# Dilated attention in a two-layer block on one core: the query tiles of each head taken in descending order

## Chip, core and metric

The kernel runs as one program on one core of a Trainium2 chip. The metric is the device time of one execution in microseconds (us), given as the median of several runs. The engines are called PE (TensorE, matrix products), DVE (VectorE), ACT (ScalarE), POOL (GpSimd) and SP (SyncE, which issues most transfers). Each engine takes its instructions strictly in the order in which they are written; they meet only at semaphores.

## The reference, cut to what matters

The reference is a chain of transformer layers over 512 tokens of width 1024. The stage that the change touches is the dilated attention of the last layer: 4 heads of width 128, and for each head three groups of queries q (three windows with dilations 1, 4 and 16) that share the keys k and the values v. For one head h and one tile of 128 query rows the kernel computes, with only the keys up to the tile's own last row:

```
for t in range(4):                       # tile of 128 query rows, n = 128 * (t + 1) keys
    z0 = q0[h, t] @ k[h, n-256:n].T      # window 0: distance 0..128   (128 keys for t = 0)
    z1 = q1[h, t] @ k[h, 0:n].T          # window 1: distance divisible by 4
    z2 = q2[h, t] @ k[h, 0:n].T          # window 2: distance divisible by 16
    z  = scale * (masked z0, z1, z2)
    p  = exp(z - max z)                  # one maximum and one sum over all three windows
    p  = (p0 + p1 + p2) / sum(p)         # n columns
    y[h, t] = p @ v[h, 0:n]
```

The result of a head is then multiplied by a gate (z3T) and goes into the output product (wout3), which sums over the heads. So tile t = 0 has one key tile, t = 3 has four.

## The kernel before

The program is one fixed list of instructions for each engine, written out by hand. Weights come in as slabs; each is split into a high part by ACT (w_hi) and a low part by POOL (w_lo, raw minus w_hi), and a product is three matmuls (high by high, high by low, low by high).

The dilated attention has 16 units, u = 48 to 63 in the program's count (U_D = 48), here unit 0 to unit 15: unit number = 4 h + position in the head. A unit passes through the engines so:

- PE, `d_logits`: three products into three of banks 0 to 5 (two sets, taken in turn). They wait for the minimum of the unit two before (semaphore at_neg).
- DVE, `unit_least` (L2448 in the trace): mask, scale and running minimum; it writes 128 x (256 + 2n) numbers into the buffer prob3 (four buffers), or 384 columns for t = 0. For t = 2 it is two instructions, since the window pieces aren't one regular pattern.
- ACT (L1916): exponential in place, with the sum.
- POOL (L704, L706): adds window 1 and 2 (n columns), then adds window 0 (at most 256 columns).
- DVE, `unit_probs` (L2460, L2462): reciprocal, then the scaling of n columns.
- PE, `attn_transposes` (L887): t + 1 transposes into bank 6.
- ACT, `copy_probs` (L1527): bank 6 to prob3T (two buffers).
- PE: t + 1 products with v into bank 7, one quarter of the bank for a query tile. They start three steps after the logits for the transposes (LAG_T = 3), four for the products (LAG_OUT = 4).
- After the four units of a head DVE multiplies bank 7 by z3T (L2476, prob_y), and makes y_hi (L2478) and y_lo (L2479). The first product of the next head into bank 7 waits for L2476 (at_y).

The loops on all engines count `step` from 0 to 15 or 19. In a step PE does logits of unit `step`, transposes of unit `step - 3`, products of unit `step - 4`. DVE takes `unit_probs` of unit `step - 2` ahead of `unit_least` of unit `step` where step % 4 is 0 or 3, and behind it otherwise. On POOL four quarters of a w_lo slab (`lo_quarter`, L564 in the trace) are written ahead of the sums of units 8, 9, 12 and 13. On ACT one split of a weight slab follows the exponential of unit 6. From step 16 on PE has no logits, and `head_products` (12 matmuls of 512 columns for a head, in parts) of the output product fill in.

The trace gives nearly all matmuls the line of the helper `mm`, L715; logits read as `banks<-k3T,q3T`, products with v as `banks<-prob3T,v`, head products as `banks<-w_hi,y_hi` and the like. Each matmul of the program whose operands are plain f32 shows as two records.

Of the kernel before, what the change touches and what calls it, by code (L numbers as in the profile page):

```python
# [26 lines left out]
P = 128  # L27
S = 512
NT = S // P
# [124 lines left out]
def head_and_tile(n):  # L154

    return 2 * (n // 8) + n % 2, n % 8 // 2
# [3 lines left out]
LAG_T, LAG_OUT = 3, 4  # L160
# [65 lines left out]
def _program(nc, A, ctx):  # L226
# [3 lines left out]
    def place(name, kib, words, dtype=F32, parts=P):  # L230
        return nc.alloc_sbuf_tensor_at(name, [parts, words], dtype, offset=SB0 + int(kib * 1024))

    def arena(name, kib, words, dtype=F32, parts=P):
        return place(name, ARENA + kib, words, dtype, parts)
# [115 lines left out]
    prob3 = [arena(f"prob3{a}", 64 + 6 * a, 3 * S) for a in range(4)]  # L350
    prob3T = [place(f"prob3T{a}", 80 + 2 * a, S) for a in range(2)]
# [188 lines left out]
    def _(pool):  # L540
# [82 lines left out]
        for u in range(32):  # L623
            h, t = head_and_tile(u)
            n = (t + 1) * P
# [70 lines left out]
        for step in range(16):  # L696
            if step in (8, 9, 12, 13):
                lo_quarter(BASE["wout3"] + 1, (8, 9, 12, 13).index(step))
            u, t = 48 + step, step % 4
            n = (t + 1) * P  # L700
            n0 = min(n, 256)
            buf = prob3[u % 4]
            pool.wait_ge(at_exp, u + 1)
            pool.tensor_tensor(buf[:, S:S + n], buf[:, S:S + n], buf[:, S + n:S + 2 * n], ALU.add).then_inc(w_sum, 1)  # L704
            pool.wait_ge(w_sum, 2 * step + 1)
            pool.tensor_tensor(buf[:, S + n - n0:S + n], buf[:, S + n - n0:S + n], buf[:, S - n0:S], ALU.add).then_inc(w_sum, 1)  # L706
# [6 lines left out]
    def _(pe):  # L713
# [168 lines left out]
        def attn_transposes(u, src, ntiles):  # L882
            pe.wait_ge(at_norm, u + 1)
            if u >= 1:
                pe.wait_ge(at_trc, u)
            for kt in range(ntiles):
                ins = pe.transpose(banks[:, 6, kt * P:(kt + 1) * P], src[:, kt * P:(kt + 1) * P], const("ident"))  # L887
            ins.then_inc(at_tr, 1)
# [28 lines left out]
        U_C, U_A, U_D = 0, 16, 48  # L917
        for step in range(16 + LAG_OUT):
            if step < 16:
                h, t = divmod(step, 4)  # L920
                attn_logits(U_C + step, lambda u: mm(banks[:, 4 + u % 2, 0:N_MEM], cqT[:, h * S + t * P:h * S + (t + 1) * P],
                                                     mkT[:, h * N_MEM:(h + 1) * N_MEM], True, True))
            if 0 <= step - LAG_T < 16:
                u = step - LAG_T
                attn_transposes(U_C + u, prob[(U_C + u) % 4], 2)
            if step >= LAG_OUT:
                u = step - LAG_OUT
                h, t = divmod(u, 4)
# [58 lines left out]
        for step in range(32 + LAG_OUT):  # L987
            if step < 32 and step % 2 == 0:
                pair_logits(step)
            if 0 <= step - LAG_T < 32:  # L990
                u = U_A + step - LAG_T
# [66 lines left out]
        for step in range(1, 8 + 2):  # L1058
# [15 lines left out]
            if step <= 8:  # L1074
                h = step - 1
# [143 lines left out]
        for step in range(4 + 1):  # L1219
            if step < 4:  # L1220
                h = step
# [6 lines left out]
            if step >= 1:  # L1228
                h = step - 1
# [110 lines left out]

        def d_logits(u):

            h, t = divmod(u - U_D, 4)
            n = (t + 1) * P
            for w in range(3):
                k0 = max(0, n - 256) if w == 0 else 0
                c0 = 256 if (w, t) == (0, 3) else 0
                ins = mm(banks[:, 3 * (u % 2) + w, c0:c0 + n - k0], q3T[:, (4 * w + h) * S + t * P:(4 * w + h) * S + (t + 1) * P],
                         k3T[:, h * S + k0:h * S + n], True, True)
            return ins  # L1350
# [14 lines left out]
        for step in range(16 + LAG_OUT):  # L1365
            if step == 17:
                head_products(0, (2,))
            if step == 18:
                pe.wait_ge(at_neg, U_D + 16)
                head_products(0, (3,))  # L1370
            if step == 19:
                head_products(1, range(2))
            if step in (1, 3):
                wait_emptied(EV_A["z3"] + (step + 1) // 2, EV_V["z3"] + (step + 1) // 2)
            if step < 16:
                attn_logits(U_D + step, d_logits)
            if 0 <= step - LAG_T < 16:
                u = U_D + step - LAG_T
                attn_transposes(u, prob3[u % 4][:, S:2 * S], (u - U_D) % 4 + 1)
            if step == 16:  # L1380
                pe.wait_ge(at_neg, U_D + 15)
                head_products(0, range(2))
            if step >= LAG_OUT:
                u = U_D + step - LAG_OUT
                h, t = divmod(step - LAG_OUT, 4)
                pe.wait_ge(at_trc, u + 1)
                if t == 0:
                    pe.wait_ge(at_y, h)
                for kt in range(t + 1):
                    ins = mm(banks[:, 7, t * P:(t + 1) * P], v3[:, kt * HALF + h * P:kt * HALF + (h + 1) * P],  # L1390
                             prob3T[u % 2][:, kt * P:(kt + 1) * P], kt == 0, kt == t)
                ins.then_inc(at_out, 1)
# [8 lines left out]
    def _(act):  # L1401
# [121 lines left out]
        def copy_probs(u, dst, n, tr=None):  # L1523
            act.wait_ge(at_tr, u + 1)
            if u >= 2:
                act.wait_ge(at_out, u - 1)
            act.activation(dst[:, 0:n], banks[:, 6, 0:n], ACT.Copy).then_inc(at_trc, 1)  # L1527

        U_C, U_A, U_D = 0, 16, 48
# [54 lines left out]
        for step in range(16 + LAG_OUT):  # L1584
            index_relus(step - 1)
            if 0 <= step - LAG_T < 16:
                u = U_C + step - LAG_T
# [3 lines left out]
            if (step - LAG_OUT) % 4 == 3 and step >= LAG_OUT:  # L1591
                h = (step - LAG_OUT) // 4
# [13 lines left out]
        for step in range(32 + LAG_OUT):  # L1606
            if 0 <= step - LAG_T < 32:
                u = U_A + step - LAG_T
# [18 lines left out]
        for step in range(8 + 2):  # L1627
# [12 lines left out]
            for n, c in enumerate((LATER, FIRST)):  # L1640
# [3 lines left out]
                if 1 <= step <= 8:  # L1644
                    h = step - 1
# [127 lines left out]
        for step in range(4 + 2):  # L1773
            if step < 4:
                h = step
# [12 lines left out]
            if step >= 2:  # L1788
                h = step - 2
# [114 lines left out]
        for step in range(16 + LAG_OUT):  # L1904
            if 0 <= step - LAG_T < 16:
                u = U_D + step - LAG_T
                copy_probs(u, prob3T[u % 2], ((step - LAG_T) % 4 + 1) * P)
            if step < 16:
                u = U_D + step
                n = (step % 4 + 1) * P  # L1910
                buf = prob3[u % 4]
                b = word_of(u)
                packed = buf[:, S - min(n, 256):S + 2 * n]
                least = b + 1 if step % 4 == 2 else b
                act.wait_ge(at_neg, u + 1)
                act.activation(packed, packed, ACT.Exp, bias=negmax[:, least:least + 1], scale=-1.0,  # L1916
                               accum_out=total[:, b:b + 1]).then_inc(at_exp, 1)
            if step == 6:
                split_hi(0, "wout3", 0)
# [4 lines left out]
    def _(dve):  # L1924
# [87 lines left out]
        U_C, U_A, U_D = 0, 16, 48  # L2012
# [45 lines left out]
        for step in range(16 + LAG_OUT):  # L2058
            index_sums(step - 2)
            if step < 16:  # L2060
                u = U_C + step
# [7 lines left out]
            if (step - LAG_OUT) % 4 == 3 and step >= LAG_OUT:  # L2069
                h = (step - LAG_OUT) // 4  # L2070
# [48 lines left out]
        for step in range(32 + LAG_OUT):  # L2119
            if step < 32:  # L2120
                u, t = U_A + step, head_and_tile(step)[1]
                n = (t + 1) * P
# [188 lines left out]
        for step in range(4 + 2):  # L2311
            if step < 4:
                h = step
# [5 lines left out]
            if step >= 2:  # L2319
                h = step - 2  # L2320
# [5 lines left out]
            if 1 <= step <= 4:  # L2326
                h = step - 1
# [11 lines left out]
            if step >= 2:  # L2339
                h = step - 2  # L2340
# [87 lines left out]
            dve.tensor_tensor(part, flat[:, 2048 + 1024 * s:3072 + 1024 * s], part, ALU.mult).then_inc(ev_v, 1)  # L2428
        dve.wait_ge(rp_Tc, 16)
        def unit_least(step):  # L2430
            u, t = U_D + step, step % 4
            n = (t + 1) * P
            n0 = min(n, 256)
            b = word_of(u)
            dve.wait_ge(at_log, u + 1)
            dve.wait_ge(at_tr, u - 3)
            buf, b0 = prob3[u % 4], 3 * (u % 2)
            if t == 3:
                parts = [(buf[:, 256:256 + 1280], flat[:, b0 * 512 + 256:b0 * 512 + 1536], dil[:])]
            elif t == 2:  # L2440
                parts = [(buf[:, S - 256:S], banks[:, b0, 0:256], dil[:, 0:256]),
                         (buf[:, S:S + 2 * n].rearrange("p (w c) -> p w c", w=2), banks[:, b0 + 1:b0 + 3, 0:n],
                          dil[:, 256:].rearrange("p (w c) -> p w c", w=2)[:, :, S - n:S])]
            else:
                parts = [(buf[:, S - n:S + 2 * n].rearrange("p (w c) -> p w c", w=3), banks[:, b0:b0 + 3, 0:n],
                          dil[:].rearrange("p (w c) -> p w c", w=5)[:, 0:5:2, 256 - n:256])]
            for i, (packed, logits, mask) in enumerate(parts):
                ins = dve.tensor_tensor_reduce(out=packed, in0=logits, in1=mask, scale=-scale_c,  # L2448
                                               scalar=3.0e38 if i == 0 else negmax[:, b:b + 1], op0=ALU.add, op1=ALU.min,
                                               accum_out=negmax[:, b + i:b + i + 1])  # L2450
                if i < len(parts) - 1:
                    link(ins)
            ins.then_inc(at_neg, 1)

        def unit_probs(step):
            u, t = U_D + step - 2, (step - 2) % 4
            n = (t + 1) * P
            b, buf = word_of(u), prob3[u % 4]
            dve.wait_ge(at_exp, u + 1)
            link(dve.reciprocal(inverse[:, b:b + 1], total[:, b:b + 1]))  # L2460
            dve.wait_ge(w_sum, 2 * (step - 1))
            dve.tensor_scalar(buf[:, S:S + n], buf[:, S:S + n], inverse[:, b:b + 1], None, ALU.mult).then_inc(at_norm, 1)  # L2462

        for step in range(16 + LAG_OUT):
# [7 lines left out]
            if (step - LAG_OUT) % 4 == 3 and step >= LAG_OUT:  # L2472
                h = (step - LAG_OUT) // 4
# [45 lines left out]
```

## Time and profile before

| | |
|---|---|
| median of 3 runs | 1568.92 us (1567.63 to 1568.95) |
| time of the profiled execution | 1567.16 us |
| its span, first to last instruction | 1565.4 us |
| PE busy | 1529.0 us, 98% |
| DVE, ACT, POOL busy | 700.2, 596.7, 693.3 us |
| granted TensorE clock | 1.0 of full speed |
| dilated attention, first logits to last head product | 1435.9 to 1491.9 us |

PE is busy for nearly the whole span, so what counts is where it waits. The stage of the change is the last 56 us but one; behind it come the second half of the output product and a gated addition.

### The profile page before, as it was taken

What the parts mean: (1) busy time and instruction counts of PE and PEld (TensorE: products, weight loads), DVE (VectorE), ACT (ScalarE), POOL (GpSimd) and SP (SyncE); (2) the same over time, 40 slices, a digit from 0 to 9 for tenths busy, and PEclk for the clock granted to TensorE, in tenths of its full rate; (3) what the DMA queues carried; (4) which work ended last, traced back from release to release, by engine and by line L of the source; (5) the groups of instructions that cost most, each with busy time, mean ns of one, the idle gap of its engine ahead of it and who ended that gap; (6) DMA issues with size and microseconds to landing.
All of it is one profiled execution on the core that took longest, in us unless ns stands there. A gap on an engine that the chain in (4) does not pass through costs nothing.

```text
span 1565.4 us, 19693 instructions
## 1 busy us (share of the span) xinstructions
PE 1529.0 (98%) x7585; PEld 1252.2 (80%) x7585; DVE 700.2 (45%) x1147; ACT 596.7 (38%) x908; POOL 693.3 (44%) x312
## 2 busy tenths in 40 slices
PE   7999999999999999999999999999999999999898
PEld 6877966868888888888888887888878888887687
DVE  4157855382243326656655005630035346445733
ACT  5353245573223315221222114422344444455452
POOL 5423365233555545534444344444432434454632
PEclk9999999999999999999999999999999999999999
DMA  7323311102333332333332225443421232322021
GB/s 233 112 75 112 105 54 48 41 21 76 87 97 100 114 108 68 108 107 86 102 107 81 108 82 70 98 106 91 126 68 54 81 108 81 95 81 81 28 69 67
DMA packets 144966, 138.26 MB, mean 88 GB/s; under 512 B 7760, under 2 KB 118224, under 8 KB 144892
## 3 DMA queue, kind: packets, MB, share of 16 engines
q1 hardware_dynamic: 140676, 130.79, 29.0%
q10 hardware_dynamic: 4216, 6.45, 1.3%
q8 instruction: 51, 0.84, 0.2%
q14 instruction: 23, 0.19, 0.0%
HBM read 135.09 MB, written 2.13 MB: 88 GB/s over the span
## 4 chain that ended last, share of the span: by engine, by line
PE 89%; DVE 3%; ACT 3%; POOL 3%; issue 1%; DMA 1%; SPq 0%; DVEq 0%; ACTq 0%; POOLq 0%
PE banks L715 86%; POOL w_lo L564 2%; PE banks L741 2%; PE banks L887 1%; DMA raw<-in_w_mem_kv 1%; ACT w_hi L1427 0%; PE banks L1303 0%; DVE prob L2448 0%; POOL prob L704 0%; DVE resid L2212 0%; ACT k L1854 0%; ACT junk L1693 0%; POOL prob L706 0%; ACT junk L1686 0%; DVE head_ms L2410 0%
## 5 line engine op out<-in xcount | busy, mean ns | idle before, releaser
L547 POOL TENSOR_TENSOR w_lo<-raw,w_hi 128x2048 fp32r<-128x2048 f32 x104 | 481.3, 4628 | 602.3 <-ACT w_hi L1427 602.3
L715 PE MATMUL banks<-h_hi,w_hi 128*128 128x512 f32 (+1 forms) x904 | 348.0, 385 | 2.4 <-DVE h_lo L1991 0.9
L715 PE MATMUL banks<-h_hi,w_lo 128*128 128x512 f32 (+1 forms) x904 | 340.4, 377 | 0.0
L715 PE MATMUL banks<-h_lo,w_hi 128*128 128x512 f32 (+1 forms) x904 | 340.1, 376 | 0.0
L1427 ACT ACTIVATE w_hi<-raw 128x2048 fp32r<-128x2048 f32 x126 | 238.8, 1896 | 214.8 <-PE banks L715 209.4
L715 PEld LDWEIGHTS banks<-h_hi,w_hi 128*128 128x128 f32 x904 | 169.9, 188 | 42.5 <-issue 9.7
L715 PE MATMUL banks<-w_hi,h_hi 128*128 128x512 f32 (+1 forms) x544 | 199.3, 366 | 0.0
L715 PE MATMUL banks<-w_hi,h_lo 128*128 128x512 f32 (+1 forms) x544 | 198.1, 364 | 0.0
L715 PE MATMUL banks<-w_lo,h_hi 128*128 128x512 f32 (+1 forms) x544 | 198.1, 364 | 0.0
L715 PEld LDWEIGHTS banks<-h_hi,w_lo 128*128 128x128 f32 x904 | 169.7, 188 | 32.2
L715 PEld LDWEIGHTS banks<-h_lo,w_hi 128*128 128x128 f32 x904 | 170.0, 188 | 29.0
L564 POOL TENSOR_TENSOR w_lo<-raw,w_hi 128x512 fp32r<-128x512 f32 x84 | 113.2, 1367 | 96.1 <-ACT w_hi L1427 91.0
L715 PEld LDWEIGHTS banks<-w_hi,h_hi 128*128 128x128 f32 x544 | 102.7, 189 | 16.7 <-issue 0.9
L715 PEld LDWEIGHTS banks<-w_hi,h_lo 128*128 128x128 f32 x544 | 102.6, 189 | 16.4
L715 PEld LDWEIGHTS banks<-w_lo,h_hi 128*128 128x128 f32 x544 | 102.7, 189 | 15.8
L2253 DVE TENSOR_TENSOR f_lo<-ff_prod,f_hi 128x512 f32 x22 | 102.8, 4675 | 4.3 <-DVE f_hi L2251 2.9
L1717 ACT ACTIVATE ff_sig<-banks 128x512 f32<-128x512 f32 x22 | 13.2, 600 | 175.8 <-PE banks L715 175.8
L1972 DVE TENSOR_REDUCE meansq<-sumsq 128x1 f32<-128x2 f32 (+4 forms) x19 | 2.9, 153 | 151.1 <-ACT junk L1686 130.4
L715 PE MATMUL banks<-w_hi,f_lo 128*128 128x512 f32 x176 | 68.5, 389 | 0.0
L715 PE MATMUL banks<-w_hi,f_hi 128*128 128x512 f32 x176 | 68.5, 389 | 0.0
L715 PE MATMUL banks<-w_lo,f_hi 128*128 128x512 f32 x176 | 68.5, 389 | 0.0
L1666 ACT ACTIVATE gate<-banks,col 128x512 f32<-128x512 f32 x24 | 16.5, 689 | 130.5 <-PE banks L715 130.5
(310 smaller groups left out, 2330.9 us busy)
## 6 DMA issues: line engine op xcount, KB each, us to landing
raw<-in_w_in SPq DMA_DIRECT2D x56, 512.0 KB, 4.0
raw<-in_w_ffn_in SPq DMA_DIRECT2D x44, 512.0 KB, 4.8
raw<-in_w_in_a SPq DMA_DIRECT2D x32, 512.0 KB, 5.7
raw<-in_w_ffn_out SPq DMA_DIRECT2D x22, 512.0 KB, 4.0
raw<-in_w_ple_gate SPq DMA_DIRECT2D x16, 512.0 KB, 4.6
raw<-in_w_in_b SPq DMA_DIRECT2D x16, 512.0 KB, 4.3
raw<-in_w_mem_kv SPq DMA_DIRECT2D x8, 512.0 KB, 5.7
raw<-in_w_out SPq DMA_DIRECT2D x8, 512.0 KB, 3.6
```

What stands on the lines that cost most here:

```text
L547: pool.tensor_tensor(slot_of(w_lo, slot), slot_of(raw, slot), slot_of(w_hi, slot).bitcast(F32), ALU.subtract).then_inc(lo_made, 1)
L564: ins = pool.tensor_tensor(w_lo[:, c], raw[:, c], w_hi[:, c].bitcast(F32), ALU.subtract)
L715: return pe.matmul(out, lhsT, rhs, start=start, stop=stop, **kw)
L741: ins = pe.transpose(banks[:, transposed_bank(name, k), t * P:(t + 1) * P], rows(t)[:, k * P:(k + 1) * P], const("ident"))
L887: ins = pe.transpose(banks[:, 6, kt * P:(kt + 1) * P], src[:, kt * P:(kt + 1) * P], const("ident"))
L1427: act.activation(slot_of(w_hi, slot, words), slot_of(raw, slot, words), ACT.Copy).then_inc(hi_made, 1)
L1666: act.activation(gate[slot][:], banks[:, 2 * slot, :], ACT.Sigmoid, bias=col[:, ds(V_BGATE + KD * (s % 3) + ft, 1)]).then_inc(ev_a, 1)
L1717: act.activation(ff_sig[:], banks[:, 2 * slot, :], ACT.Sigmoid).then_inc(ev_a, 1)
L1972: link(dve.tensor_reduce(meansq[:, c], pieces, AX_X, ALU.add))
L2253: dve.tensor_tensor(lo, ff_prod[:], hi.bitcast(F32), ALU.subtract).then_inc(lo_ffn, 1)
```

## The change

The position in the head is kept, but the query tile that stands in it is reversed on every engine: position 0 is now t = 3 (four key tiles), position 3 is t = 0. The transposes and copies of a unit have the matching sizes, the wait for bank 7 stands ahead of t = 3, now the first of a head, and the number where the minimum of t = 2 lies follows that tile. Buffers, lags, the order of `unit_probs` and `unit_least`, and the steps of the w_lo quarters are as before. No instruction is added or removed.

```diff
@@ POOL
             if step in (8, 9, 12, 13):
                 lo_quarter(BASE["wout3"] + 1, (8, 9, 12, 13).index(step))
-            u, t = 48 + step, step % 4
+            u, t = 48 + step, 3 - step % 4
@@ PE, d_logits
-            h, t = divmod(u - U_D, 4)
+            h, t = (u - U_D) // 4, 3 - (u - U_D) % 4
@@ PE, loop over steps
-                attn_transposes(u, prob3[u % 4][:, S:2 * S], (u - U_D) % 4 + 1)
+                attn_transposes(u, prob3[u % 4][:, S:2 * S], 4 - (u - U_D) % 4)
...
-                h, t = divmod(step - LAG_OUT, 4)
+                h, t = (step - LAG_OUT) // 4, 3 - (step - LAG_OUT) % 4
                 pe.wait_ge(at_trc, u + 1)
-                if t == 0:
+                if t == NT - 1:
                     pe.wait_ge(at_y, h)
@@ ACT
-                copy_probs(u, prob3T[u % 2], ((step - LAG_T) % 4 + 1) * P)
+                copy_probs(u, prob3T[u % 2], (4 - (step - LAG_T) % 4) * P)
...
-                n = (step % 4 + 1) * P
+                n = (4 - step % 4) * P
...
-                least = b + 1 if step % 4 == 2 else b
+                least = b + 1 if step % 4 == 1 else b
@@ DVE, unit_least
-            u, t = U_D + step, step % 4
+            u, t = U_D + step, 3 - step % 4
@@ DVE, unit_probs
-            u, t = U_D + step - 2, (step - 2) % 4
+            u, t = U_D + step - 2, 3 - (step - 2) % 4
```

The start of the stage on PE, before (prob_182 to prob_185 are the four buffers of prob3, prob3T_186 is the first of the two prob3T):

```order
L715 MATMUL banks<-k3T,q3T 128x128 x3
L715 MATMUL banks<-k3T,q3T 128x256 x4
L715 MATMUL banks<-k3T,q3T 128x384 x2
L715 MATMUL banks<-k3T,q3T 128x256
L715 MATMUL banks<-k3T,q3T 128x512 x2
L887 MATMUL banks<-sq,prob_182 128x128
L715 MATMUL banks<-k3T,q3T 128x128 x3
L887 MATMUL banks<-sq,prob_183 128x128 x2
L715 MATMUL banks<-prob3T_186,v_167 128x128
```

The same place on PE with the change:

```order
L715 MATMUL banks<-k3T,q3T 128x256
L715 MATMUL banks<-k3T,q3T 128x512 x2
L715 MATMUL banks<-k3T,q3T 128x256
L715 MATMUL banks<-k3T,q3T 128x384 x2
L715 MATMUL banks<-k3T,q3T 128x256 x3
L715 MATMUL banks<-k3T,q3T 128x128 x3
L887 MATMUL banks<-sq,prob_182 128x128 x4
L715 MATMUL banks<-k3T,q3T 128x256
L715 MATMUL banks<-k3T,q3T 128x512 x2
L887 MATMUL banks<-sq,prob_183 128x128 x3
```

Between the first transposes and the first product with v there now stand the logits of a unit with four key tiles, where those of a unit with one key tile stood.

The border of two heads on POOL (units 7, 8 and 9; the border at units 11, 12 and 13 is alike), before:

```order
L704 TENSOR_TENSOR prob_185<-prob_185 128x512
L706 TENSOR_TENSOR prob_185<-prob_185 128x256
L564 TENSOR_TENSOR w_lo<-raw,w_hi 128x512
L704 TENSOR_TENSOR prob_182<-prob_182 128x128
L706 TENSOR_TENSOR prob_182<-prob_182 128x128
L564 TENSOR_TENSOR w_lo<-raw,w_hi 128x512
L704 TENSOR_TENSOR prob_183<-prob_183 128x256
```

The same place on POOL with the change:

```order
L704 TENSOR_TENSOR prob_185<-prob_185 128x128
L706 TENSOR_TENSOR prob_185<-prob_185 128x128
L564 TENSOR_TENSOR w_lo<-raw,w_hi 128x512
L704 TENSOR_TENSOR prob_182<-prob_182 128x512
L706 TENSOR_TENSOR prob_182<-prob_182 128x256
L564 TENSOR_TENSOR w_lo<-raw,w_hi 128x512
L704 TENSOR_TENSOR prob_183<-prob_183 128x384
```

The quarters of w_lo stand where they stood by number, but now ahead of and right behind the sums of the head's largest unit.

## Rows read from the trace of the kernel before

**Rows 1.** The page: busy time of each engine, and the chain that ended last.

```profile
PE 1529.0 (98%) x7585; PEld 1252.2 (80%) x7585; DVE 700.2 (45%) x1147; ACT 596.7 (38%) x908; POOL 693.3 (44%) x312
...
PE 89%; DVE 3%; ACT 3%; POOL 3%; issue 1%; DMA 1%; SPq 0%; DVEq 0%; ACTq 0%; POOLq 0%
```

**Rows 2.** Windows: start:end, length, busy us of PE, PEld, DVE, ACT, POOL; clock, DMA.

```profile
1435.89:1444.25 8.36, 7.35 (x34) 4.90 (x33) 5.79 (x14) 5.45 (x9) 2.84 (x5) 1.00 0.36 126
1444.25:1454.85 10.60, 9.96 (x56) 7.17 (x55) 7.40 (x22) 8.24 (x14) 7.36 (x10) 1.00 0.01 2
1454.85:1466.19 11.34, 9.62 (x54) 7.22 (x55) 9.68 (x22) 5.83 (x13) 8.71 (x10) 1.00 0.00 0
1466.19:1477.54 11.35, 10.40 (x54) 7.61 (x55) 9.68 (x22) 5.84 (x13) 8.72 (x10) 1.00 0.30 92
1477.54:1491.88 14.34, 13.06 (x70) 10.93 (x71) 6.67 (x12) 3.36 (x9) 2.07 (x2) 1.00 0.00 2
```

**Rows 3.** Timeline of PE: start us, us; in brackets idle before and releaser.

```profile
1442.87 0.33 PE L887 MATMUL banks<-sq,prob 128*128 128x128 f32 x1
...
1450.25 2.31 PE L715 MATMUL banks<-k3T,q3T 128*128 128x256 f32 x6
1452.40 0.27 PE L887 MATMUL banks<-sq,prob 128*128 128x128 f32 x1
1452.51 1.06 PE L715 MATMUL banks<-prob3T,v 128*128 128x128 f32 x8
1453.41 0.83 PE L715 MATMUL banks<-k3T,q3T 128*128 128x128 f32 x6
...
1457.29 0.55 PE L887 MATMUL banks<-sq,prob 128*128 128x128 f32 x3 [0.68 <-DVE prob L2462]
...
1466.19 0.46 PE L715 MATMUL banks<-prob3T,v 128*128 128x128 f32 x2 [1.04 <-DVE prob_y L2476]
...
1479.98 0.55 PE L887 MATMUL banks<-sq,prob 128*128 128x128 f32 x3 [1.28 <-DVE prob L2462]
...
1486.28 0.40 PE L715 MATMUL banks<-w_hi,y_hi 128*128 128x512 f32 x1
...
1491.06 0.39 PE L715 MATMUL banks<-w_hi,y_hi 128*128 128x512 f32 x1
```

**Rows 4.** Timeline of DVE.

```profile
1438.29 0.55 DVE L2448 CUSTOM_DVE_ANT_1 prob<-banks,dil 128x384 f32<-128x384 f32 x1
...
1445.69 0.42 DVE L2462 TENSOR_SCALAR prob<-prob,inverse 128x384 f32<-128x384 f32 x1 [0.94 <-POOL prob L706]
...
1452.60 1.49 DVE L2448 CUSTOM_DVE_ANT_0 prob<-banks,dil 128x1280 f32<-128x1280 f32 x1 [0.94 <-PE banks L715]
...
1456.00 1.23 DVE L2462 TENSOR_SCALAR prob<-prob,inverse 128x384 f32<-128x384 f32 x1
...
1458.70 0.65 DVE L2462 TENSOR_SCALAR prob<-prob,inverse 128x512 f32<-128x512 f32 x1
...
1463.01 1.02 DVE L2462 TENSOR_SCALAR prob<-prob,inverse 128x256 f32<-128x256 f32 x1 [0.75 <-POOL prob L706]
```

**Rows 5.** Timeline of ACT: one exponential and the read of its sum.

```profile
1454.14 1.36 ACT L1916 ACTIVATE prob<-prob,negmax 128x1280 f32<-128x1280 f32 x1
1455.40 0.18 ACT L1916 ACTIVATION_READ_ACCUMULATOR prob<-prob,negmax 128x1 f32 x1
```

**Rows 6.** Timeline of POOL around the border of heads 1 and 2.

```profile
1455.67 1.35 POOL L704 TENSOR_TENSOR prob<-prob 128x512 f32<-128x512 f32 x1 [1.68 <-ACT prob L1916]
1457.09 0.73 POOL L706 TENSOR_TENSOR prob<-prob 128x256 f32<-128x256 f32 x1
1457.79 1.27 POOL L564 TENSOR_TENSOR w_lo<-raw,w_hi 128x512 fp32r<-128x512 f32 x1
1459.03 0.63 POOL L704 TENSOR_TENSOR prob<-prob 128x128 f32<-128x128 f32 x1
...
1462.89 0.99 POOL L704 TENSOR_TENSOR prob<-prob 128x384 f32<-128x384 f32 x1
```

## The prediction

> **What bounds the kernel now.** I read the page first: PE is busy for 98% of the span and carries 89% of the chain that ended last [rows 1]. No work is added or taken away, so the change can only move PE's waits in its own stage. I therefore cut the stage into stretches, each from one head's first product with v to the next head's [rows 2]: 8.36 us to fill the pipeline, then 10.60, 11.34 and 11.35 us for three heads, and 14.34 us from the last head's first product to the last head product. The reader is to see that POOL and DVE are as loaded as PE there: 8.7 us of POOL and 9.7 us of DVE in an 11.34 us head. The first of the three has no quarter of w_lo on POOL and is 0.74 us shorter.
>
> Then the timeline of PE in that stretch [rows 3]. A row's length holds an overlap with the next one, so I take start to start. A four-key-tile unit costs 2.15 us of logits (1450.25 to 1452.40), 0.11 us for one transpose (1452.40 to 1452.51), 0.90 us for four key tiles of products (1452.51 to 1453.41). Its other sizes, read in the same way, give logits of 0.67, 1.30, 1.72 and 2.15 us for t = 0 to 3, transposes of 0.11, 0.25, 0.35 and 0.45, and products of 0.30, 0.45, 0.67 and 0.90: 9.3 us for a head. The rest of a head is waits: for the scaled probabilities (0.68 us, and 1.28 in the last head) and for the reading of bank 7 (1.04 us).
>
> Who makes these waits is on DVE and POOL. A scaling of 384 columns takes 0.42 us, but 1.23 us at 1456.00 [rows 4]. POOL's add ran from 1455.67 to 1457.02 [rows 6], and the scaling ended 0.21 us behind it. The scaling of 256 columns at 1463.01 had waited for POOL's sums, and took 1.02 us since POOL had already gone on at 1462.89 to the next unit's add, which ended at 1463.88. The scaling of 512 columns at 1458.70 ended at 1459.35, 0.29 us behind the w_lo quarter [rows 4, 6]. So **a scaling that finds POOL at work ends 0.1 to 0.3 us after POOL's instruction, by its size**, and where POOL has its next one ready, it gets there first. In the other direction the add at 1459.03 took 0.63 us, though 0.32 us of DVE's scaling were still to come; the same add without DVE beside it takes 0.46, so 0.17 us were lost.
>
> The Trainium skill says in "SBUF — State Buffer", section "SBUF: two separate sides", that such pairs of DVE and GpSimd instructions share a port pair under an exclusive lock, which whoever starts first holds for its whole instruction. The trace agrees for DVE. For POOL the rule would charge the whole 0.32 us and the row only 0.17. That difference comes three times on the path below (0.15 us each); by the rule the sum would be about 3.3 us, by the row it is 2.9.
>
> **The change, part by part.** I walked the new order through the engines with these start-to-start costs, each instruction starting at the later of its engine's last and its releaser's end. The hand-over times are read from neighbouring rows: 0.04 us DVE to ACT, 0.08 to POOL, 0.10 POOL to DVE, 0.06 to PE, 0.14 behind a copy or bank-7 read. The same walk over the old order ends at 1491.86 us, where the trace has 1491.88; none of POOL's 36 starts is off by more than 0.12 us. All matmuls, the minimum, exponential and sums exist in the trace in every size; only their neighbours are new.
>
> *Fill.* DVE's first minimum starts at 1438.29 as before [rows 4], since it waits for the gate, not PE (the larger logits from 1435.89 take 2.31 us and are ready at 1438.20). From here the larger unit costs: minimum 1.49 (1439.78); exponential with its sum 1.44, being 1.36 plus 0.18 less 0.10 of overlap [rows 5] (1441.28); POOL's sums 1.28 + 0.07 + 0.73 [rows 6] (1443.43). POOL goes straight on to unit 1's add, 1.00 us, to 1444.40. The scaling, ready at 1443.53, ends at 1444.69. PE's first transposes start at 1444.75, against 1442.87 [rows 3]: 1.88 us late. Up to the first product there then lie 0.45 (four transposes) + 2.15 (logits of unit 4) + 0.35, and no longer 1.38 us with a small wait: another 1.57. First product at 1447.70: **+3.45 us**.
>
> *Head 1.* PE's 9.3 us plus waits of 0.31 and 0.66 us for scalings: 10.28 against 10.60, **-0.32**. The wait for bank 7 is gone here, as the small last unit makes its reading early.
>
> *Head 2.* A scaling of t = 0 meets POOL's 512-column add (0.84 us of wait on PE). That of t = 3 (unit 8) is ready at 1464.39; POOL went to its w_lo quarter at 1464.26, holds it to 1465.53, and PE waits 1.01 us. Bank 7 costs 0.48. 11.63 against 11.34: **+0.29**.
>
> *Head 3.* The large unit now opens the head on DVE too: its minimum comes behind y_lo and a scaling (1471.2), its exponential ends at 1474.17, POOL's sums to 1476.42, then the quarter again ahead of the scaling, to 1477.66. PE waits 2.2 us. Behind it unit 13's sums end at 1479.60 and its scaling loses to the next add: 1.8 us. PE has 8.6 us of work in this stretch (no logits in its last step, 1.40 us of head products in), with 0.14 us of other wait 12.72 against 11.35: **+1.37**.
>
> *Tail.* The last units are small, so all that follows the last head's first product is PE's own work: products 0.90 + 0.67 + 0.45 + 0.30, transposes 0.23 + 0.11, 14 head-product tiles (the other two lie in head 3) of 0.70 us: seven of them take 4.78 us from 1486.28 to 1491.06 [rows 3], 0.68 each, and I add 0.02 for the first of a group. Together 12.46 us. Before, this stretch was 14.34 us with the 1.28 us wait: **-1.88**. The last y_lo (1489.8) lies 2 us ahead of the products that need it.
>
> The w_lo quarters end at 1477.7, 17 us before wout3's second half wants them, and PE is 89% of the chain [rows 1], all of it just behind the stage, so the shift passes on whole. Sum: 3.45 - 0.32 + 0.29 + 1.37 - 1.88 = **+2.9 us**, on the profiled execution 1567.16 to 1570.1. The median of the runs is 1.8 us above the profiled one; I add the shift to it: 1568.92 + 2.9 = **1571.8 us**, 0.18% more. What a measurement of this kernel can tell from no change is about 0.2%, 3.1 us.
>
> Where the walk is soft are the races between DVE and POOL. Moving each cost by 0.04 us at random moves the sum between 2.0 and 3.1 us, in 1 of 30 cases over 4. Without POOL's share of the collisions (a lower bound) it is 2.4.
>
> **The rivals.** *The collisions go worse (slower side).* If the misses of head 3 already come in head 2, at units 8 and 9, that head too takes 12.7 us: +1.1, and one more missed race is another 0.5 to 0.9. Against it speaks that PE has logits to do in head 2; for it that POOL's quarter at unit 9 is ready at once. It decides when the scaling of unit 8 ends after 1466.5. Total +4.0 to +4.9, 1573.4.
>
> *The scaling slips in first.* If DVE gets through between POOL's instructions at units 0, 8, 12 and 13, the first transposes come 0.67 us earlier, the others 0.94, 0.94 and 0.5: 3.0 us less, nothing is left, 1568.9. The row at 1463.01 speaks against it: DVE was released by the very instruction after which POOL went on, and came second.
>
> *Only the tail counts (faster).* PE never waits once the pipeline is full: heads of 9.3, 9.3 and 8.6 us, a fill of +3.45 and the tail of -1.88 give 3.45 - 1.3 - 2.0 - 2.8 - 1.9 = -4.5 us, 1564.4. It needs POOL's quarters to fall into POOL's waits for exponentials alone and every scaling in time, so it is decided by the waits at units 8 and 12 being under 0.3 us. POOL's 8.7 us of work in a head, nearly all in one chain with DVE and ACT, speaks against it.
>
> **How the numbers follow.** The forecast has 0.50, the worse collisions 0.27, the scaling first 0.16, the faster one 0.04, and 0.03 for nothing at all. The forecast's own spread passes 3.1 us in a quarter of its cases (0.13), giving slower 0.41, within 0.2% 0.55, faster 0.04. The range holds the forecast, most of the worse collisions and most of the case without them: 1569.3 to 1573.8.
>
> **What would show it.** PE's first L887 near 1444.7 and first product with v near 1447.7; stretches of the heads near 10.3, 11.6 and 12.7 us; scalings of 512 columns of about 1.2 to 1.4 us at units 0, 8 and 12; a wait of about 2 us ahead of the transposes of unit 12; no PE wait behind the last head's first product. The prediction is wrong if the scalings of 512 columns last 0.5 us, or if PE waits for minima (its logits) at the borders of heads, which the walk has nowhere after the start.

## The result and the profile after

| | before | changed |
|---|---|---|
| median | 1568.28 us (8 runs) | 1574.15 us (8 runs) |
| lowest to highest | 1567.19 to 1569.19 | 1571.55 to 1575.62 |
| profiled execution, span | 1565.4 us | 1571.8 us |
| granted clock, mean over the span, single runs | 1.000 to 0.999 | 0.999 to 0.996 |

The ratio is 1.0037 (95% interval 1.0028 to 1.0046): 5.9 us slower, twice the 2.9 us that I forecast, and above my range, which ended at 1573.8. The direction was right. The page of the changed kernel shows PE busy for 4 us more, though not one instruction was added [rows 1]:

```profile
PE 1533.0 (98%) x7585; PEld 1255.6 (80%) x7585; DVE 703.0 (45%) x1147; ACT 597.3 (38%) x908; POOL 694.4 (44%) x312
```

Here is the stage of the changed kernel in windows, cut as in [rows 2]: fill, three heads, tail. The columns are the same; the third number from the right is the granted clock.

```profile
1436.38:1449.92 13.54, 11.13 (x38) 6.59 (x37) 7.86 (x18) 7.23 (x11) 6.06 (x8) 0.87 0.21 78
1449.92:1460.12 10.20, 9.61 (x56) 7.23 (x55) 7.96 (x19) 7.69 (x13) 5.41 (x7) 1.00 0.01 2
1460.12:1471.74 11.62, 9.78 (x57) 7.18 (x55) 9.61 (x21) 5.99 (x13) 8.82 (x10) 1.00 0.00 0
1471.74:1485.22 13.48, 10.03 (x54) 8.02 (x55) 11.51 (x25) 6.21 (x13) 10.46 (x12) 0.93 0.26 78
1485.22:1498.23 13.01, 13.01 (x67) 11.18 (x66) 4.30 (x9) 1.92 (x6) 0.00 (x0) 0.94 0.01 1
```

Heads 1 and 2 came out at 10.20 and 11.62 us, where the prediction had 10.28 and 11.63. The fill took 13.54 (predicted 11.81), head 3 13.48 (12.72), the tail 13.01 (12.46), and these three are the stretches in which the granted clock isn't 1.00. PE's timeline of the changed kernel shows where:

```profile
1442.09 0.91 PE L715 MATMUL banks<-k3T,q3T 128*128 128x128 f32 x6
1445.26 0.75 PE L887 MATMUL banks<-sq,prob 128*128 128x128 f32 x4 [2.26 <-DVE prob L2462]
1445.80 3.96 PE L715 MATMUL banks<-k3T,q3T 128*128 128x256 f32 x6
...
1479.99 0.66 PE L887 MATMUL banks<-sq,prob 128*128 128x128 f32 x4 [0.79 <-DVE prob L2462]
1480.49 0.39 PE L715 MATMUL banks<-prob3T,v 128*128 128x128 f32 x2
1482.55 0.55 PE L887 MATMUL banks<-sq,prob 128*128 128x128 f32 x3 [1.68 <-DVE prob L2462]
...
1483.94 0.63 PE L715 MATMUL banks<-w_hi,y_hi 128*128 128x512 f32 x1
...
1485.22 1.74 PE L715 MATMUL banks<-prob3T,v 128*128 128x128 f32 x8
```

The logits of a unit with four key tiles take 3.96 us behind a wait of 2.26 us, and took 2.31 before [rows 3]. A head-product matmul takes 0.63 us (0.40 in [rows 3]), and eight records of products with v 1.74 us (1.06). Windows around the two places, with the same columns as above:

```profile
1442.99:1445.26 2.27, 0.01 (x1) 0.00 (x1) 0.86 (x3) 1.15 (x4) 2.11 (x4) 1.00 0.01 4
1445.26:1449.60 4.34, 4.34 (x11) 2.38 (x12) 1.72 (x6) 1.30 (x3) 2.85 (x5) 0.61 0.00 0
...
1480.49:1482.55 2.06, 0.38 (x5) 0.20 (x3) 0.85 (x2) 0.60 (x1) 1.90 (x4) 1.00 0.79 159
1482.55:1485.22 2.67, 2.67 (x9) 2.17 (x10) 2.56 (x7) 1.08 (x3) 1.88 (x3) 0.63 0.70 270
1485.22:1487.03 1.81, 1.81 (x10) 1.77 (x9) 0.50 (x3) 0.00 (x0) 0.00 (x0) 0.60 0.04 9
```

The reader is to see that PE is idle for most of the two stretches 1442.99:1445.26 and 1480.49:1482.55 while the clock is still granted in full, and busy throughout in the rows behind them, at a clock that has meanwhile fallen (a mean of about 0.6 over stretches that hold a piece at 1.00 and some 3 us at 0.50). The price is read from start to start. Up to the first product the fill is 1.73 us above the walk. The two head-product tiles take 2.37 us (1482.85 to 1485.22) where 1.40 were counted, and the products 1.50 (1485.22 to 1486.72) where 0.90 were: 1.57. Together 3.3 us of 5.9, and the other 2.6 are the order of the work.

### The profile page after: what moved, and what is told of

It reads as the page before. It is cut to its first block, busy times and chain, and to the rows that moved or that the text cites. A ratio compares the mean times of both kernels' runs of the same rounds, so it can differ in the third digit from the quotient of the medians.

```text
span 1571.8 us, 19693 instructions
## 1 busy us (share of the span) xinstructions
PE 1533.0 (98%) x7585; PEld 1255.6 (80%) x7585; DVE 703.0 (45%) x1147; ACT 597.3 (38%) x908; POOL 694.4 (44%) x312
## 4 chain that ended last, share of the span: by engine, by line
PE 89%; ACT 3%; DVE 3%; POOL 2%; issue 2%; DMA 0%; ACTq 0%; DVEq 0%; POOLq 0%
PE banks L715 86%; PE banks L741 2%; POOL w_lo L564 1%; PE banks L887 1%; ACT w_hi L1427 1%; POOL prob L704 1%; PE banks L1303 0%; DMA onehot<-in_c_onehot 0%; DVE resid L2212 0%; ACT k L1854 0%; DVE prob L2448 0%; POOL prob L706 0%; ACT junk L1693 0%; ACT junk L1686 0%; DVE head_ms L2410 0%
```

## Experiments

The stage starts at 1435.89 us in the earliest trace and at 1437.87 in the latest, though nothing ahead of it was changed in these kernels but e12_fill_up (more on that at the end), so I compare the stage itself in the traces: from the first logits to the last head product. Its end is the start of the last unit's products with v, plus those, plus ten tiles of head products, which take 7.07 us (1484.81 to 1491.88 before). Before it is 55.99 us, in the changed kernel 61.85. The *walk* is the prediction's, extended with each edit and always at full clock. Its 58.7 us for the changed kernel and 55.8 for before are the measure for the rows below (the prediction's own walk of before ended at 1491.86 us, a stage of 55.97). Each stage is that of one traced execution. Medians and ratios are to runs of the kernel before on the same chip.

| kernel | walk | stage | clock below 1 in the stage | median | ratio, 95% interval |
|---|---|---|---|---|---|
| changed | 58.7 | 61.85 | fill, end | 1574.15 | 1.0037 (1.0028 to 1.0046) |
| e1_fill | 58.7 | 60.24 | end | 1573.20 | 1.0032 (1.0020 to 1.0044) |
| e5_fill2 | 58.7 | 58.72 | no | 1570.12 | 1.0013 (1.0004 to 1.0022) |
| e2_hp | 58.3 | 60.04 | fill, end | 1573.05 | 1.0028 (1.0017 to 1.0039) |
| e3_both | 58.3 | 58.29 | no | 1571.21 | 1.0017 (1.0008 to 1.0026) |
| e9_wait | 58.0 | 59.71 | fill | 1572.55 | 1.0028 (1.0017 to 1.0038) |
| e6_addd | 56.1 | 58.59 | end | 1569.88 | 1.0010 (1.0001 to 1.0019) |
| e7_daaa | 58.2 | 59.60 | fill | 1571.43 | 1.0023 (1.0014 to 1.0032) |
| e4_dve | 56.7 | 59.97 | fill, end | 1571.33 | 1.0018 (1.0009 to 1.0027) |
| e10_dddd | 55.1 | 55.13 | no | 1569.78 | 1.0003 (0.9994 to 1.0012) |
| e11_aaaa | 54.9 | about 55.2 | no | 1566.62 | 0.9990 (0.9981 to 0.9999) |
| e8_best | 52.6 | 52.77 | no | 1564.31 | 0.9981 (0.9972 to 0.9990) |

**e1_fill: work in the first wait.**

```diff
+            if step == 3:
+                for _ in range(9):
+                    mm(banks[:, 7, :], h_hi[:, 0:P], h_hi[:, 0:S], True, True)
             if 0 <= step - LAG_T < 16:
                 u = U_D + step - LAG_T
                 attn_transposes(...)
```

> Changed kernel, with nine matmuls of 512 columns (results overwritten later, bank 7) put on PE ahead of the first transposes, where PE waits 2.3 us. Clock theory (the long wait lowers the granted clock, and the logits behind it run slowly: 3.96 us in place of 2.31): those logits take 2.3 us again and the whole is 1.5 to 1.9 us faster than the changed kernel, so about 4.3 us over before. Rival (the loss is all order of work: waits and collisions): the added matmuls hide at best, so 5.9 us over before, or more.

PE's timeline of e1_fill:

```profile
1444.10 2.33 PE L715 MATMUL banks<-h_hi 128*128 128x512 f32 x9
1446.66 0.66 PE L887 MATMUL banks<-sq,prob 128*128 128x128 f32 x4 [0.23 <-DVE prob L2465]
1447.15 2.31 PE L715 MATMUL banks<-k3T,q3T 128*128 128x256 f32 x6
```

The logits are back at 2.31 us, and the stage is 1.61 us shorter, by matmuls that compute nothing. The clock fell at the end of the stage alone. In the ratio to before the difference to the changed kernel is within the intervals, and the median is 0.95 us lower where 1.5 to 1.9 were expected. So the gain rests on one trace each, and a fall can also stay away by itself (e10_dddd below); the next run has more than that to show.

**e5_fill2: work in the second wait too.** This is e1_fill with, in step 16 ahead of the transposes of unit 13:

```diff
+            if step == 16:
+                pe.wait_ge(at_neg, U_D + 15)
+                pe.wait_ge(at_lo, 9)
+                for _ in range(6):
+                    mm(banks[:, 2, :], y3_hi[:, 0:P], y3_hi[:, 0:S], True, True)
```

> Kernel e1_fill, with six more matmuls of 512 columns (results overwritten later, bank 2) in step 16 ahead of the transposes of unit 13, where PE waits 1.68 us. The order of the real work is as in the changed kernel. Clock theory: the granted clock stays at 1.0, the two head-product tiles behind take 1.4 us in place of 2.4 and the next products with v 0.9 in place of 1.5, so the stage is 1.6 us shorter than in e1_fill (58.7 us from first logits to last head product, against 60.2). Rival (the slow matmuls there come from something else beside them, transfers or POOL): no shorter than e1_fill.

PE's timeline of e5_fill2:

```profile
1480.35 1.64 PE L715 MATMUL banks<-y_hi 128*128 128x512 f32 x6
1482.29 0.55 PE L887 MATMUL banks<-sq,prob 128*128 128x128 f32 x3 [0.30 <-DVE prob L2470]
...
1484.06 1.05 PE L715 MATMUL banks<-prob3T,v 128*128 128x128 f32 x8
```

The products with v take 1.05 us and no longer 1.74. The stage is 58.72 us, the walk's number for the changed order without any fall of the clock. So 3.1 of the 5.9 us were the clock, and the order itself cost 2.7. Here the runs show it too: the intervals of e5_fill2 and the changed kernel don't touch, and the medians are 4.0 us apart. Eight of the eleven runs lie between 1569.85 and 1570.22 us and three between 1571.62 and 1571.93, where none of the changed kernel's eight is under 1571.55. The traced run, 1571.66, is one of the three, with a fall of the clock 280 us ahead of the stage and none in it. Transfers ran beside these matmuls here as in the changed kernel (their share was 0.60 from 1482.60 to 1485.22), so transfers alone don't make the matmuls slow.

**e2_hp and e3_both: real work in the second wait.** Head products of tiles 0 and 1 move ahead of the transposes of unit 13; e3_both adds the fill of e1_fill.

```diff
+            if step == 16:
+                pe.wait_ge(at_neg, U_D + 15)
+                head_products(0, range(2))
             if 0 <= step - LAG_T < 16:
                 ... attn_transposes ...
-            if step == 16:
-                pe.wait_ge(at_neg, U_D + 15)
-                head_products(0, range(2))
```

> Changed kernel, with the first two tiles of head products taken ahead of the transposes of unit 13 in step 16, so that real work fills PE's second long wait. Clock theory: 1.4 us saved by the order and 1.2 to 1.6 us more because the head products and the next products with v no longer run at a lowered clock: 2.6 to 3.0 us faster than the changed kernel, 2.9 to 3.3 over before. Rival (order alone): 1.4 us faster, 4.5 over before, and the matmuls behind the transposes still show 0.56 to 0.63 us each.

> Both edits together. Clock theory: the two costs are separate and add, 4.3 to 4.8 us faster than the changed kernel, 1.1 to 1.6 over before. Rival (order alone): 1.4 us faster than the changed kernel, 4.5 over before.

e2_hp came out nearer to the rival. Its stage is 1.81 us shorter than the changed kernel's and its median 1.1 us lower, 4.4 over before, and head-product matmuls still take 0.63 us. But the slow matmuls are no longer those behind the filled wait. The clock fell one wait earlier, behind the wait of 1.98 us for unit 12, as PE's timeline of e2_hp shows.

```profile
1481.39 1.11 PE L887 MATMUL banks<-sq,prob 128*128 128x128 f32 x4 [1.98 <-DVE prob L2462]
```

My 1.4 us for the order was too high as well. In the walk it is 0.4, because the first product of the last head then waits for the reading of bank 7 (0.62 us in e3_both). The table's 58.3 us are the walk with this wait in it. The expectations went by 1.4 us, which is 57.3, so that e3_both meets 58.3 is no forecast that came true. e3_both had no fall in the stage, not even behind a wait of 1.99 us for unit 12. "Order alone, 1.4 us" is refuted by it, but so is my sum of 4.3 to 4.8: the stage is 3.6 us shorter than the changed kernel's, the median 2.9 lower.

**e9_wait: the old order with a long wait.** The kernel before, and nothing else but:

```diff
+            if step == 3:
+                pe.wait_ge(at_norm, U_D + 3)
             if 0 <= step - LAG_T < 16:
```

> The kernel before, old order throughout, with one wait added: PE's first transposes also wait for the scaling of unit 2, so that PE is idle for 3.3 us there. The walk without any effect of the clock gives a stage of 58.0 us against 55.8. Clock theory: the granted clock falls to half behind this wait although no tile is reversed, for 3 to 4 us, and what runs there takes up to twice its time; 58.0 to 59.7 us, since later waits can hide a part. Rival (the fall belongs to the descending order or its larger logits): clock 1.0 throughout, 58.0 us.

PE's timeline of e9_wait, with the logits of a unit with one key tile in the second row:

```profile
1446.17 0.43 PE L887 MATMUL banks<-sq,prob 128*128 128x128 f32 x1 [3.12 <-DVE prob L2464]
1446.40 1.49 PE L715 MATMUL banks<-k3T,q3T 128*128 128x128 f32 x6
```

1.49 us, against 0.83 in [rows 3], and a stage 1.7 us above the walk. Two windows of e9_wait behind the wait, at the lower clock:

```profile
1447.00:1448.00 1.00, 1.00 (x7) 1.00 (x6) 0.07 (x1) 1.00 (x1) 0.00 (x0) 0.50 0.00 0
1448.00:1449.00 1.00, 1.00 (x6) 0.91 (x5) 0.49 (x2) 0.91 (x4) 0.66 (x1) 0.50 0.00 0
```

None of the eight runs is less than 3.6 us above the lowest of before, where the wait alone is worth 2.2 by the walk. So the fall needs neither the descending order nor large logits; it follows the wait.

**e6_addd and e7_daaa: one part of the change alone.** All tile numbers go through one function, here for heads 1 to 3 descending (e6_addd) or head 0 alone (e7_daaa).

```diff
+ASCENDING = (0,)          # e7_daaa: (1, 2, 3)
+def tile_of(n):
+    return n % 4 if n // 4 in ASCENDING else 3 - n % 4
```

> The change on heads 1 to 3 only; head 0 keeps its ascending order. The walk gives 0.3 us over before, and waits of 2.2 and 1.8 us ahead of the transposes of units 12 and 13, so by the clock theory another 1.6 us: 1.9 over before, stage 57.7 us. Rival (all of the loss is in the descending order of every head alike): three quarters of 5.9 us, 4.4 over before.

> The change on head 0 only. The walk gives 2.4 us over before, with the 2.6 us wait ahead of the first transposes, behind which the clock falls (1.7 us more); the end of the stage is as before and the clock doesn't fall there. 4.1 over before, stage 60.0 us. Rival (as for e6_addd): a quarter of 5.9 us, 1.5 over before.

The loss doesn't spread evenly, so the rival is out. Head 0 alone costs 3.6 us of stage, with a median 2.7 us over before. The other three cost 2.6 in the profiled execution, where the clock fell already behind the 1.98 us wait for unit 12 and stayed low longer than I had counted; its runs have a median 1.1 us over before. By the walk, the order of heads 1 to 3 costs only 0.3.

**e4_dve: DVE's order reversed as well.**

```diff
-            probs_first = step % 4 in (0, 3)
+            probs_first = step % 4 in (1, 2)
```

> Changed kernel, with DVE's order reversed as well: unit_probs ahead of unit_least in steps with step % 4 of 1 and 2 in place of 0 and 3. The walk through the engines gives 2.1 us less waiting than the changed kernel, with the first wait of 2.6 us still there and one of 1.8 us ahead of unit 13's transposes. If the walk's account of waits holds and the clock falls at the same two places, it is about 2 us faster than the changed kernel, 3.8 over before. Rival (DVE's order doesn't matter, POOL's chain sets the heads): within 0.5 us of the changed kernel.

The stage is 1.88 us shorter than the changed kernel's, with both falls of the clock still there, and the median 2.8 lower. That `probs_first` was fitted to the ascending sizes, and that the change left it as it was, is thus a part of the 2.6 us of order.

**e8_best, e10_dddd, e11_aaaa: the order with its surroundings fitted.** The three have these edits in common, found by walking variants; they differ in the heads that descend: 1 to 3, all, none.

```diff
-            if step in (8, 9, 12, 13):
+            if step in (8, 11, 12, 15):          # POOL, w_lo quarters
...
-            probs_first = step % 4 in (0, 3)
+            probs_first = step % 4 in (3,)       # DVE
...
+            if step == 16:                       # PE, ahead of the transposes
+                pe.wait_ge(at_neg, U_D + 15)
+                head_products(0, range(3))
             if step == 17:
-                head_products(0, (2,))
-            if step == 18:
                 pe.wait_ge(at_neg, U_D + 16)
                 head_products(0, (3,))
...
-            if step == 16:                       # PE, behind the transposes
-                pe.wait_ge(at_neg, U_D + 15)
-                head_products(0, range(2))
```

> Kernel e6_addd (head 0 ascending, heads 1 to 3 descending) with three edits that the walk points to: unit_probs ahead of unit_least in steps with step % 4 of 3 alone, the w_lo quarters ahead of units 8, 11, 12 and 15, and the first three tiles of head products ahead of the transposes of unit 13, the fourth in step 17. The walk gives a stage of 52.6 us against 55.8 before, with no PE wait over 1.1 us, so no fall of the clock: 3.2 us faster than before. Rival (the walk misses waits once several orders change together): no faster than before.

> The three edits of e8_best with all four heads descending, as in the change. Walk 55.1 us, plus 1.7 us for the clock behind the 2.3 us wait ahead of the first transposes: stage 56.8 us, 0.8 over before. Rival (with the three edits the order doesn't matter): 52.8 us as e8_best, 3 us faster than before.

> The three edits of e8_best with all four heads ascending, as before. Walk 54.9 us, no fall of the clock: 0.9 us faster than before. If e8_best owes its gain to the three edits alone, this is 3 us faster; if to the descending heads alone, not faster at all; by the walk it needs both.

e8_best is faster than both kernels, 0.9981 (0.9972 to 0.9990) of before. The stage is 3.2 us shorter, and its longest wait is the 0.88 us that the kernel before has too. With the same three edits, no head descending gives 0.9990, all four 1.0003. The gain needs both, and descending in head 0 spoils it. The traces show where. Against e11_aaaa, e8_best has 2.8 us less from head 2's first product with v to the end (22.70 for 25.51), 0.8 less in the two stretches ahead of that, and 1.2 more in the fill, which holds the logits of head 1's large first unit. Against e8_best, e10_dddd has 2.33 us more in the fill (11.85 for 9.52) and 0.03 in all the rest. So the descending order isn't bad in itself: it is good at the end of the stage, and bad at its start, where PE has nothing else to do until the first unit has passed through four engines.

e10_dddd missed its expectation in the trace in one respect. PE waited 2.26 us ahead of the first transposes, as in the changed kernel, and the clock did not fall. Windows of e10_dddd up to that wait's end and behind it:

```profile
1437.71:1446.59 8.88, 6.47 (x25) 3.89 (x23) 6.02 (x12) 5.92 (x8) 3.21 (x4) 1.00 0.35 119
1446.59:1450.60 4.01, 4.01 (x22) 2.95 (x23) 2.46 (x5) 1.80 (x4) 2.87 (x5) 1.00 0.00 0
```

Up to that wait the instructions are those of the changed kernel. So the same wait has a fall behind it in one execution and none in another. The times fit that: two of e10_dddd's eleven runs lie near 1566.5 us, three near 1568.0 and six near 1570.0. The traced one, 1568.11, is of the middle group and has one fall, ahead of the stage. The highest group would then have both, but none of its runs has a trace.

**e12_fill_up: the wait far ahead of the stage.** Every kernel of this study but e12_fill_up has another such place in the mLSTM stage. One row of the kernel before and one of e3_both, of the same eight records behind the same wait:

```profile
1157.04 2.42 PE L715 MATMUL banks<-qk2T 128*128 128x512 f32 x8 [2.49 <-DVE wts L2318]
```

```profile
1157.10 4.07 PE L715 MATMUL banks<-qk2T 128*128 128x512 f32 x8 [2.49 <-DVE wts L2321]
```

The traces of e1_fill, e2_hp, e3_both, e5_fill2, e10_dddd and e11_aaaa have the fall there, the other seven with the wait have not. Where a kernel's times lie in two groups, the traced run is of the upper one in e5_fill2 and e11_aaaa, which have the fall, and of the lower one in before and e8_best, which have none. e7_daaa's is of its upper one, with a fall elsewhere (last section). The 25 runs of before beside e9_wait split 10 to 15 into 1567.1 to 1567.8 us and 1568.5 to 1569.3, with mean clocks of 1.000 and 0.999 (once 0.998). The edit, on e8_best:

```diff
+                if h == 1:
+                    for _ in range(4):
+                        mm(banks[:, 4, :], qk2T[:, 4 * S:4 * S + P], qk2T[:, 0:S], True, True)
                 if h:
                     pe.wait_ge(m_w, h)
```

> Kernel e8_best, with four plain f32 matmuls of 512 columns (results overwritten later, bank 4) put on PE some 280 us ahead of the dilated attention, in the wait of 2.49 us for the weights of the mLSTM stage's second head (near 1157 us). The times of e8_best lie in two groups, near 1564.1 and 1565.95 us, those of the kernel before near 1567.2 and 1569.1. If the upper group is the executions in which the clock falls behind that wait, all times lie near 1564.1 and the median is 1564.2, 4.5 us faster than before. Rival (the two groups come from somewhere else, a transfer for example): two groups as before, or both later.

The median was 1565.01 us, ratio 0.9981 (0.9972 to 0.9990), so not better than e8_best: the added matmuls last longer than the wait and cost some 0.7 us. Two of eleven times still lie in the upper group (1566.6 and 1566.7), against five of eleven in e8_best. Two of eleven and five of eleven don't differ by more than chance can do, so it isn't shown that the edit made the upper group rarer, and the expectation that it would be gone failed. These two runs may have had a fall elsewhere, but neither has a trace.

## Why the prediction was wrong

- **The fill, "0.45 (four transposes) + 2.15 (logits of unit 4) + 0.35", +3.45 us.** This is the step that failed first. The wait ahead of the transposes was there (2.6 us in the walk, by the expectations of e4_dve and e7_daaa; 2.26 in the row, 2.5 from start to start), and the transposes started 8.88 us behind the first logits, where the walk had 8.86. But the 2.15 us was a price from [rows 3], taken where PE had no such wait ahead of it. At half clock it was 3.8 us. Measured fill: +5.18 in place of +3.45.
- **The tail, "all that follows is PE's own work: 12.46 us", -1.88 us, and the two head-product tiles of head 3.** The same mistake. I had computed two waits of 2.2 and 1.8 us in a row and then priced what follows at full clock; 1.57 us were missing. Measured tail: 14.34 to 13.01, -1.33.
- **Heads 1 and 2, -0.32 and +0.29 us.** Measured -0.40 and +0.28. The price for a scaling that loses to POOL held. DVE's row for unit 8 in the changed kernel, and POOL's quarter that it waited for:

```profile
1466.70 1.25 DVE L2462 TENSOR_SCALAR prob<-prob,inverse 128x512 f32<-128x512 f32 x1
```

```profile
1466.40 1.28 POOL L564 TENSOR_TENSOR w_lo<-raw,w_hi 128x512 fp32r<-128x512 f32 x1
```

  The scaling ends at 1467.95, 0.27 us behind the quarter, as 0.29 us in [rows 4, 6]. Unit 12's lasted 1.24 us. Unit 0's lasted 0.78 and not "1.2 to 1.4", but it too ended 0.29 us behind POOL's add, so the sum had it right.
- **Head 3, +1.37 us.** Without the 0.97 us of slow clock in it, it took 12.5 and not 12.72 us: +1.2. The waits were distributed otherwise (0.98, 0.79 and 1.68 us for units 11, 12 and 13, where I had 0.1, 2.2 and 1.8). In e1_fill, with the same order of the real work, they were 0, 1.98 and 1.68 us, nearly the walk's. The two traces differ in one race: unit 11's scaling of 128 columns starts 0.04 us ahead of POOL's 512-column add in the changed kernel and takes 1.40 us, to 0.09 behind it; in e1_fill it starts 0.05 us ahead and takes 0.28.
- **The sum.** Without the clock it is 2.6 us (2.7 in e5_fill2) for a forecast of 2.9. With it, 5.9.
- **The rivals.** "The collisions go worse" gave about the right time for a reason that didn't occur: head 2 took 11.62 us, not 12.7. The other three didn't occur either. None of the rivals was a lower clock.
- **What I had seen and not asked about.** "The median of the runs is 1.8 us above the profiled one" stands in the prediction as a constant to be added. It is in all likelihood the same mechanism, in the kernel before: a fall of the clock ahead of the stage in about half the executions, which the profiled one didn't have. No trace of before from its upper group exists; e5_fill2's and e11_aaaa's stand in for it, and e12_fill_up didn't settle it. A clock row of 1.00 in one trace said nothing about the other executions.

The Trainium skill says in "TensorE: Matmul & The Clock Gate", section "What's actually happening", that PE's granted clock has two levels, 1.2 and 2.4 GHz, and that where it changes varies between runs of one kernel. The traces agree: in slices of 1 us every kernel here shows 1.00 or 0.50 with mixtures only at the borders, and behind the same wait of 2.49 us, with the same instructions around it, six traces of thirteen show the fall and seven don't.

## What to carry to other kernels

Where a change makes a wait of some two microseconds on a busy PE, or two shorter ones close together, price the work behind it at both clock levels, and look at whether useful matmuls can stand in the wait: here 3.1 us of stage were won back by fifteen that computed nothing. In this pipeline through four engines the shortest stage, 52.77 us, began with a small unit and ended with one, and it took an order on each engine that fits the sizes in between. And where the runs of a kernel lie in two groups, find out which one the trace belongs to before taking durations from it.

## What the runs showed of the hardware

- Behind waits of 1.98 (e2_hp, e6_addd), 2.26, 2.49 and 3.12 us, and behind pairs of waits of 0.70 and 1.63, 0.79 and 1.68 or 1.98 and 1.68 us with little work between, PE ran at 0.50 of its clock for some 3 us (in e6_addd for about 7 us). At half clock six records of a 128 x 512 logits unit took 3.96 us for 2.31, a 512-column matmul 0.63 for 0.40.
- In the dilated attention waits of up to 1.4 us that stood alone had no fall behind them in any trace. But e7_daaa has one near 317 us, where sixteen records took 4.07 us behind a wait of 0.56 us, and 2.38 us behind the same wait in the kernel before. So the length of the last wait alone doesn't tell. PE's row of e7_daaa:

```profile
317.73 4.07 PE L722 MATMUL banks<-stick_a,bv 128*64 128x512 f32 x16 [0.56 <-POOL stick_a L608]
```

- It isn't certain: e10_dddd's trace had none behind 2.26 us, those of e3_both and e5_fill2 none behind 1.99 us, and seven of thirteen traces none behind 2.49 us. What decides between them is open.
- A POOL instruction that starts while DVE's scaling still runs is lengthened by less than what DVE has left (0.17 of 0.32 us in [rows 4, 6]), while a scaling that starts behind POOL's instruction ends only after it. Starting 0.04 or 0.05 us ahead of it decides nothing by itself: unit 11's scaling lost the one time and won the other.
